# Delta rule on Trainium2: first convolution taps on ScalarE, query products on GpSimd, another order of late SiLUs

## The chip, the cores and the metric

The kernel runs on one core of a Trainium2 chip. The core has five engines that work side by side, each with its own instruction stream: TensorE (PE, matrix products into PSUM), VectorE (DVE), ScalarE (ACT, activation functions), GpSimd (POOL) and SyncE (SP, which here issues the transfers). They meet only at semaphores. The metric is the device time of one launch in microseconds (us), as the median over runs.

## What is computed

Two transformer-like blocks over 512 tokens of width 1024. The change sits in the first one, in front of its gated delta rule. There a projection gives queries, keys and values for eight heads of 128; each goes through a causal convolution of four taps over time and a SiLU; queries and keys are then brought to unit length.

```python
qkv = jax.nn.silu(causal_dwconv(jnp.concatenate([dn_q, dn_k, dn_v], axis=-1), dn_conv_w[l]))
q_a = l2_norm(qkv[..., :DN_QK].reshape(B, S, DN_HEADS, DN_DK))
k_a = l2_norm(qkv[..., DN_QK:2 * DN_QK].reshape(B, S, DN_HEADS, DN_DK))
v_a = qkv[..., 2 * DN_QK:].reshape(B, S, DN_HEADS, DN_DV)
...
o_a = gated_delta_rule(q_a, k_a, v_a, g_a, beta_a)
```

The delta rule works in chunks of 64 tokens. For each chunk and head a matrix `eye + a_mat` (unit lower triangular, made of the keys' products, their decay and beta) is inverted, then a state of 128x128 is carried from chunk to chunk, and the queries read it. Everything behind it (latent attention, the feed-forward part, the whole second block) needs its output.

## The kernel before, in words

Data stand transposed: channels on the 128 partitions, the 512 tokens along the free axis, so one head is one tile of 128x512. `ar` is an array of 50 such tiles; heads of Q are tiles 0 to 7, of K 8 to 15, of V 16 to 23. PSUM has eight banks of 128x512.

Projections. Weights come in panels of 128x2048, each of which serves two projections. SyncE loads a panel into `raw`, ScalarE makes its high part (`L1271`, "cast"), GpSimd the low part, the difference (`L2449`, four pieces, "split"), and each projection is 24 matmuls of 128x512, three for each of eight parts (`L398` to `L400`). There is room for two split panels; a panel's cast may start when TensorE has finished the panel two before. The functions `ahead` and `split` put these casts and splits into the streams of ScalarE and GpSimd in front of the first instruction that waits for a later step of TensorE: so where in a stream a wait on TensorE stands decides where a cast stands.

Convolutions. "Conv n" is the n-th in the order `QKV_ORDER`: n = 0 to 7 are keys, 8 to 15 queries, 16 to 23 values. VectorE computes it out of the bank of projection n: first tap `L1814` (a multiply by a column), three further taps `L1816`; the last one frees the bank. ScalarE then applies the SiLU in place (`conv_silu`, `L1402`), GpSimd squares the tile if n < 16 (`L2491`), TensorE sums the squares over the partitions (`L466`, the l2 sums), ScalarE takes logarithm and exponential of the sum (`rstds`, `L1335` and `L1338`), and VectorE multiplies (`unit_heads`, `L1943`), four heads a group: groups 0 and 1 are keys, 2 and 3 queries ("query products").

Beside this run the other parts of the delta rule. For t = 0 to 3 (pairs of chunks, "turns"), TensorE makes the running decays and the keys' products (`gb`, `kk`), VectorE masks them (`L1975`), ScalarE takes exponentials (`L1431`, `L1432`), VectorE multiplies (`L1983`), and conv 11 + t closes the turn. `unit_inverses` on VectorE inverts all 32x32 diagonal blocks at once: transposes in (`L1827`), 30 steps of two instructions (`L1836`, `L1837`) with other work woven in at every sixth step, copies, transposes back (`L1842`). Two masked products (`L2005`) hand the result to TensorE as XTR. `inverse_steps` then join 32x32 blocks to 64 and 128: x0 (transpose, TensorE `L656`, copied by ScalarE `L1448`), p5 (`L664`, copied `L1452`), x5 and xt5 (`L671`, `L675`, subtracted by VectorE), p6 and xt6, with GpSimd's masks (`L2505`, `L2506`, `L2509`) as further operands. Between two of these groups TensorE weaves three parts (nine matmuls) of projection 21 and later ones, and behind them the query-key products `kq`, which need all query products.

Banks. TensorE takes banks in turn out of a set: all eight first, only 0 to 5 while the inverses use 6 and 7. It may write a bank only when its last reader is done. By this turn the l2 sum of conv 10 falls on the bank of projection 15 (read by conv 15), that of conv 12 on the bank of projection 16, and projection 19 on the bank of projection 18.

The order of each stream is the order in which the code is written; nothing is reordered when it runs.

## Time and profile before

| | |
|---|---|
| median of 3 runs | 2207.74 us (2206.78 to 2209.82) |
| profiled execution | 2212.4 us, its span 2210.6 us |
| TensorE busy | 2060.6 us (93%) |
| VectorE busy | 935.7 us (42%) |
| GpSimd busy | 974.8 us (44%) |
| ScalarE busy | 798.7 us (36%) |
| mean granted clock of TensorE | 0.968 of full speed |

The page of the profile gives these for one execution, on the time axis of its span. Busy times overlap. Of the chain of work that ended last, TensorE has 83%, VectorE 9%, ScalarE 3% and GpSimd 2%. In the page's 40 slices of 55 us TensorE is busy for 9 tenths or more in most; the fourth and fifth slice (166 to 276 us), where the inverses and joining steps run, show 6 and 8 tenths, with a granted clock of 8 tenths in both. A wait is put down to the line that released it; the stretch of the change lies between 110 and 262 us.

### The profile page before, as it was taken

The numbers are of one execution on the slowest core, as the hardware profiler recorded it, in microseconds if no ns is written. First come the engines' busy times: TensorE is split into PE (matmuls) and PEld (weight loads), VectorE is DVE, ScalarE is ACT, GpSimd is POOL, SyncE is SP. The second block draws the span as 40 slices with busy tenths as digits, with TensorE's granted clock in tenths as the row PEclk, the third lists the DMA queues.
The fourth block names the chain that finished last, engine by engine and source line by source line (L and its number), as shares of the span: only waits on it lengthen the run. The fifth ranks groups of instructions, "written<-read, shape, count | busy, mean of one in ns | idle before, by whom it ended". The sixth has DMA issues, their size and how long they took to land.

```text
span 2210.6 us, 26367 instructions
## 1 busy us (share of the span) xinstructions
PE 2060.6 (93%) x10214; PEld 1652.1 (75%) x10214; DVE 935.7 (42%) x1531; ACT 798.7 (36%) x1049; POOL 974.8 (44%) x758
## 2 busy tenths in 40 slices
PE   6996899998999998999999798998999899999998
PEld 3684787785677886888888576875877687888886
DVE  2579545774543134222200577445943452111101
ACT  3454224236555234222222453333224643222221
POOL 3532442554312454655466364002442255555663
PEclk9998899999999999999999799998999999999999
DMA  6211104631101232222222311001222222222231
GB/s 286 77 51 45 39 20 163 231 125 57 53 32 50 96 134 76 97 98 102 103 98 101 119 58 58 2 30 58 96 76 77 76 93 80 97 101 103 84 113 76
DMA packets 25898, 194.96 MB, mean 88 GB/s; under 512 B 3120, under 2 KB 3376, under 8 KB 4912
## 3 DMA queue, kind: packets, MB, share of 16 engines
q1 hardware_dynamic: 25776, 193.29, 23.8%
q8 instruction: 82, 1.34, 0.2%
q14 instruction: 40, 0.33, 0.0%
HBM read 189.09 MB, written 4.19 MB: 87 GB/s over the span
## 4 chain that ended last, share of the span: by engine, by line
PE 83%; DVE 9%; ACT 3%; POOL 2%; issue 2%; DMA 1%; SPq 0%; ACTq 0%; DVEq 0%; POOLq 0%
PE ps L398 22%; PE ps L399 22%; PE ps L400 22%; PE ps L466 2%; POOL W L2449 2%; ACT W L1271 1%; PE ps L496 1%; DVE ar L1816 1%; PE ps L836 1%; PE ps L891 1%; DVE ar L1842 1%; PE ps L600 1%; PE ps L823 1%; DVE ar L1916 1%; DVE ar L1797 1%
## 5 line engine op out<-in xcount | busy, mean ns | idle before, releaser
L2449 POOL TENSOR_TENSOR W<-raw,W 128x512 fp32r<-128x512 f32 x588 | 775.4, 1319 | 1027.2 <-ACT W L1271 990.9
L398 PE MATMUL ps<-hH,W 128*128 128x512 f32 x1648 | 662.8, 402 | 48.7 <-DVE ar L1816 9.8
L400 PE MATMUL ps<-hH,W 128*128 128x512 f32 x1648 | 648.8, 394 | 0.0
L399 PE MATMUL ps<-arR,W 128*128 128x512 f32 x1392 | 543.5, 390 | 0.0
L1271 ACT CAST W<-raw 128x2048 fp32r<-128x2048 f32 x147 | 280.9, 1911 | 582.3 <-PE ps L400 554.9
L398 PEld LDWEIGHTS ps<-hH,W 128*128 128x128 f32 x1648 | 314.2, 191 | 134.0 <-issue 58.2
L400 PEld LDWEIGHTS ps<-hH,W 128*128 128x128 f32 x1648 | 314.1, 191 | 67.3
L399 PE MATMUL ps<-xL,W 128*128 128x512 f32 x848 | 337.0, 397 | 0.0
L399 PEld LDWEIGHTS ps<-arR,W 128*128 128x128 f32 x1392 | 262.4, 189 | 54.4 <-issue 0.2
L398 PE MATMUL ps<-arR,W 128*128 128x512 f32 x592 | 231.3, 391 | 3.3 <-DVE ar L1899 3.3
L400 PE MATMUL ps<-arR,W 128*128 128x512 f32 x592 | 230.9, 390 | 0.0
L399 PEld LDWEIGHTS ps<-xL,W 128*128 128x128 f32 x848 | 163.5, 193 | 33.8 <-issue 2.2
L398 PEld LDWEIGHTS ps<-arR,W 128*128 128x128 f32 x592 | 111.5, 188 | 27.3 <-DVE ar L1899 3.8
L400 PEld LDWEIGHTS ps<-arR,W 128*128 128x128 f32 x592 | 111.6, 188 | 23.3
L1816 DVE SCALAR_TENSOR_TENSOR ar<-ps,cols,ar 128x511 f32<-128x511 f32 (+1 forms) x130 | 97.4, 749 | 4.6
L466 PE MATMUL ps<-ar,cm 128*128 128x512 f32 x172 | 81.2, 618 | 13.8 <-DVE ar L1816 6.7
L1814 DVE TENSOR_SCALAR ar<-ps,cols 128x512 f32<-128x512 f32 x46 | 35.9, 779 | 105.7 <-PE ps L400 105.2
L1275 ACT CAST arR<-ar 128x512 fp32r<-128x512 f32 x74 | 45.9, 621 | 81.1 <-DVE ar L2420 31.3
L466 PEld LDWEIGHTS ps<-ar,cm 128*128 128x128 f32 x172 | 32.6, 196 | 53.8 <-issue 33.4
L1916 DVE SCALAR_TENSOR_TENSOR ar<-ar,st 128x512 f32<-128x512 f32 x56 | 59.3, 1058 | 2.0
L2414 DVE TENSOR_TENSOR ps<-ps,wide 128x512 f32<-128x512 f32 x22 | 15.4, 700 | 101.0 <-PE ps L400 88.4
L2418 DVE TENSOR_TENSOR ps<-ps,wide 128x512 f32<-128x512 f32 x22 | 15.4, 700 | 94.6 <-PE ps L400 94.6
(380 smaller groups left out, 2275.9 us busy)
## 6 DMA issues: line engine op xcount, KB each, us to landing
raw<-panels_dram SPq DMA_DIRECT2D x147, 1024.0 KB, 4.8
ar<-ada_dram SPq DMA_DIRECT2D x12, 2048.0 KB, 11.1
xT<-xT_dram SPq DMA_DIRECT2D x2, 2048.0 KB, 8.1
out_dram<-xT SPq DMA_DIRECT2D x8, 512.0 KB, 2.6
xT<-out_dram SPq DMA_DIRECT2D x1, 2048.0 KB, 7.7
wide<-wide_dram SPq DMA_DIRECT2D x1, 1024.0 KB, 4.8
cm<-cm_dram SPq DMA_DIRECT2D x1, 832.0 KB, 30.5
ar<-lora_dram SPq DMA_DIRECT2D x1, 512.0 KB, 3.2
```

The source lines that it names most:

```text
L398: mm(out, lhs[0], rhs[0], start=first, stop=False)
L399: mm(out, lhs[0], rhs[1], start=False, stop=False)
L400: return mm(out, lhs[1], rhs[0], start=False, stop=final)
L466: ins = mm(pst(name, i), sel[k] if isinstance(sel, list) else const(sel), sq, start=(k == 0), stop=(k == len(squares) - 1))
L496: ins = turn(pst((name, "turn", i))[:, c], tile(smt[i % 4])[:, c], const("ident"))
L600: ins = mm(heads4((what, t, hf))[:, h % HALF, :], tile(K0 + h)[:, c], tile((K0 if what == "kk" else Q0) + h)[:, c], start=True, stop=True)
L1271: link(nc.scalar.copy(W[:, n % SPLIT, 0, :], raw[:, n % RAW, :]), panel_high, n + 1)
L1275: link(nc.scalar.copy(dst, src), done, value)
L1814: link(ts(out, src, taps[-1], bias, ALU.mult, ALU.add if bias is not None else ALU.bypass))
L1816: ins = stt(out[:, j:S], src[:, 0:S - j], taps[n - 1 - j], out[:, j:S], ALU.mult, ALU.add)
L1916: ins = stt(acc, tile(ADA_BASE[i] + k), st[:, k:k + 1], acc, ALU.mult, ALU.add)
L2449: ins = tt(W[:, n % SPLIT, 1, c], raw[:, n % RAW, c], W[:, n % SPLIT, 0, c].bitcast(F32), ALU.subtract)
```

## The change

It does four things.

1. The first tap of conv 11 to 18 moves from VectorE to ScalarE (`conv_tap`, a multiply by a column, out of PSUM). VectorE's three further taps wait for it. Taps 11 to 14 stand at the end of the four turns; taps 15 and 16 behind SiLU 14; taps 17 and 18 one ahead of SiLU 17, one behind it.
2. The eight query products move from VectorE to GpSimd, behind its squares; between the fourth and fifth stands the split of a panel, and the split of the panel after that now comes behind the eighth, ahead of the masks, whose wait for the query products is gone.
3. On ScalarE the first query rates (logarithms and exponentials of group 2) now stand ahead of SiLU 16.
4. On ScalarE SiLU 19 and 20 now stand behind the joining steps' copies of x0 and p5, not ahead of them.

```diff
@@ -1403,6 +1403,11 @@
                     if n in SPLIT_AFTER:
                         ahead(act, "qkv", QKV_ORDER[n + 1])
 
+                def conv_tap(n):
+                    i = QKV_ORDER[n]
+                    filled(act, "qkv", i)
+                    link(nc.scalar.mul(tile(Q0 + i), pst("qkv", i), col("conv", 4 * i + 3)), sem("conv_tap"), n - 10)
+
                 def unit_rstds(g):
                     logarithm_next()
                     rstds("l2", range(4 * g, 4 * g + 4), (28, 29, 30, 31), 1.0, sem("l2_rstd"), sem("qk_normed"),
@@ -1430,16 +1435,22 @@
                         act.wait_ge(sem("gb_masked"), n)
                         link(af(pair(ATT + 2 * t, hf), pair(ATT + 2 * t, hf), ACT.Exp), sem("gdn_decay"), n)
                         link(af(spare(2 * t + hf), heads4(("gb", t, hf)), ACT.Exp), *read(("gb", t, hf)))
+                    conv_tap(11 + t)
                 act.wait_ge(sem("gc_dve"), 1)
                 link(af(sm4[:, EGC, :, :], sm4[:, GC, :, :], ACT.Exp))
                 link(af(sm4[:, KDEC, :, 0:8], sm4[:, KDEC, :, 0:8], ACT.Exp), sem("gc_act"), 1)
-                for n in range(11, 17):
+                for n in range(11, 15):
                     conv_silu(n)
+                conv_tap(15)
+                conv_tap(16)
+                conv_silu(15)
                 unit_rstds(2)
+                conv_silu(16)
+                conv_tap(17)
                 conv_silu(17)
+                conv_tap(18)
                 unit_rstds(3)
-                for n in range(18, 21):
-                    conv_silu(n)
+                conv_silu(18)
 
                 def inverse_steps(t):
 
@@ -1459,8 +1470,8 @@
                     yield
 
                 for n, _ in enumerate(inverse_steps(0)):
-                    if n == 3:
-                        conv_silu(21)
+                    if n in (0, 1, 3):
+                        conv_silu(19 + (n + 1) // 2)
                 for n, _ in enumerate(inverse_steps(1)):
                     if n == 1:
                         conv_silu(22)
@@ -1807,11 +1818,14 @@
                         else:
                             link(stt(dst(j), t, shift(j), h.bitcast(F32), ALU.add, ALU.subtract), *norm_step("low", name, j))
 
-            def causal_conv(job, i, out, taps, done, value, bias=None):
+            def causal_conv(job, i, out, taps, done, value, bias=None, tapped=None):
 
                 src = pst(job, i)
                 n = len(taps)
-                link(ts(out, src, taps[-1], bias, ALU.mult, ALU.add if bias is not None else ALU.bypass))
+                if tapped:
+                    dve.wait_ge(*tapped)
+                else:
+                    link(ts(out, src, taps[-1], bias, ALU.mult, ALU.add if bias is not None else ALU.bypass))
                 for j in range(1, n):
                     ins = stt(out[:, j:S], src[:, 0:S - j], taps[n - 1 - j], out[:, j:S], ALU.mult, ALU.add)
                     if j < n - 1:
@@ -1945,7 +1959,8 @@
                 def conv(n):
                     i = QKV_ORDER[n]
                     filled(dve, "qkv", i)
-                    causal_conv("qkv", i, tile(Q0 + i), [col("conv", 4 * i + j) for j in range(4)], None, None)
+                    causal_conv("qkv", i, tile(Q0 + i), [col("conv", 4 * i + j) for j in range(4)], None, None,
+                                tapped=(sem("conv_tap"), n - 10) if 11 <= n <= 18 else None)
 
                 for n in range(8):
                     conv(n)
@@ -1995,11 +2010,9 @@
                 conv(17)
                 for _ in range(6):
                     next(units)
-                unit_heads(2)
                 conv(18)
                 for _ in range(6):
                     next(units)
-                unit_heads(3)
                 next(units)
                 for hf in range(2):
                     link(tt(pair(XTR, hf), pair(AX, hf), bm(const("same32")), ALU.mult), sem("gdn_xtr"), 1 + hf)
@@ -2491,9 +2504,14 @@
                     link(tt(tile(24 + n % 4), x, x, ALU.mult), sem("l2_sq"), n + 1)
                     if n in SPLIT_AFTER:
                         ahead(pool, "qkv", QKV_ORDER[n + 1])
+                for n in range(8, 16):
+                    if n == 12:
+                        ahead(pool, "qkv", QKV_ORDER[18])
+                    pool.wait_ge(sem("l2_rstd"), n + 1)
+                    x = tile(Q0 + QKV_ORDER[n])
+                    link(tt(x, x, tile(28 + n % 4), ALU.mult), sem("qk_normed"), n + 1)
                 ahead(pool, "qkv", QKV_ORDER[19])
                 pool.wait_ge(consts_in, 16)
-                pool.wait_ge(sem("qk_normed"), 16)
                 pool.wait_ge(sem("ax_ready"), 1)
 
                 def masks(t):
```

GpSimd, from its last squares of the heads to its first masks (L2491 and L2504 squares, L2449 and L2462 splits, L2506 and L2524 masks), before:

```order
L2491 TENSOR_TENSOR ar<-ar 128x512 x4
L2449 TENSOR_TENSOR W<-raw,W 128x512 x8
L2506 TENSOR_TENSOR ar<-ar,cm 128x512 x2
L2509 TENSOR_TENSOR ar<-ar,cm 128x512 x2
L2449 TENSOR_TENSOR W<-raw,W 128x512 x4
L2505 TENSOR_TENSOR ar<-ar,cm 128x512
```

and now:

```order
L2504 TENSOR_TENSOR ar<-ar 128x512 x4
L2512 TENSOR_TENSOR ar<-ar 128x512 x4
L2462 TENSOR_TENSOR W<-raw,W 128x512 x4
L2512 TENSOR_TENSOR ar<-ar 128x512 x4
L2462 TENSOR_TENSOR W<-raw,W 128x512 x4
L2524 TENSOR_TENSOR ar<-ar,cm 128x512 x2
L2527 TENSOR_TENSOR ar<-ar,cm 128x512 x2
L2462 TENSOR_TENSOR W<-raw,W 128x512 x4
```

L2512 are the query products, four and four, with one panel's split between them and one behind them; before, both splits stood together.

ScalarE, from SiLU 13 and 14 on to the second group of query rates (L1402 SiLU, L1325 table for logarithms, L1335 and L1338 rates, L1271 cast), before:

```order
L1271 CAST W<-raw 128x2048
L1402 ACTIVATE ar<-ar 128x512 x2
L1325 ACT_TABLE_LOAD
L1335 ACTIVATE ar<-ps,cols 128x512 x4
L1338 ACTIVATE ar<-ar,cols 128x512 x4
L1271 CAST W<-raw 128x2048
L1402 ACT_TABLE_LOAD
L1402 ACTIVATE ar<-ar 128x512
L1325 ACT_TABLE_LOAD
L1335 ACTIVATE ar<-ps,cols 128x512 x4
L1338 ACTIVATE ar<-ar,cols 128x512 x4
```

and now (L1409 is the tap):

```order
L1402 ACTIVATE ar<-ar 128x512 x4
L1271 CAST W<-raw 128x2048
L1409 ACTIVATE ar<-ps,cols 128x512 x2
L1402 ACTIVATE ar<-ar 128x512
L1325 ACT_TABLE_LOAD
L1335 ACTIVATE ar<-ps,cols 128x512 x4
L1338 ACTIVATE ar<-ar,cols 128x512 x4
L1402 ACT_TABLE_LOAD
L1402 ACTIVATE ar<-ar 128x512
L1271 CAST W<-raw 128x2048
L1409 ACTIVATE ar<-ps,cols 128x512
L1402 ACTIVATE ar<-ar 128x512
```

Two taps follow the cast, the rates of group 2 come behind one SiLU instead of two, and the next cast stands in front of tap 17.

ScalarE, from the SiLU of conv 18 to the first joining steps (L1448 and L1459 copies of x0, L1452 and L1463 of p5, L1457 and L1468 of p6), before:

```order
L1402 ACT_TABLE_LOAD
L1402 ACTIVATE ar<-ar 128x512
L1271 CAST W<-raw 128x2048
L1402 ACTIVATE ar<-ar 128x512 x2
L1448 COPY ar<-ps 128x512 x2
L1452 COPY ar<-ps 128x512 x2
L1271 CAST W<-raw 128x2048
L1457 COPY ar<-ps 128x512 x2
```

and now:

```order
L1325 ACT_TABLE_LOAD
L1335 ACTIVATE ar<-ps,cols 128x512 x4
L1338 ACTIVATE ar<-ar,cols 128x512 x4
L1402 ACT_TABLE_LOAD
L1402 ACTIVATE ar<-ar 128x512
L1271 CAST W<-raw 128x2048
L1459 COPY ar<-ps 128x512 x2
L1402 ACTIVATE ar<-ar 128x512
L1463 COPY ar<-ps 128x512 x2
```

The SiLUs of conv 19 and 20 stood both ahead of the copies of x0; now one stands behind these and one behind those of p5.

## Rows read from the trace of the kernel before

**Rows 1.** Waits of TensorE, 165 to 262 us: total us, times, longest us

```profile
PE ps L398 <- DVE ar L1816: 9.8, 1, 9.8
PE ps L466 <- DVE ar L1816: 6.7, 1, 6.7
PE ps L656 <- DVE ar L2005: 4.3, 2, 3.3
PE ps L664 <- ACT ar L1448: 3.3, 1, 3.3
```

**Rows 2.** Timeline of VectorE, 165 to 219 us: start, us, line, operation

```profile
165.05 2.32 DVE L1816 SCALAR_TENSOR_TENSOR ar<-ps,cols,ar 128x511 f32<-128x511 f32 x3
...
180.81 0.75 DVE L1814 TENSOR_SCALAR ar<-ps,cols 128x512 f32<-128x512 f32 x1
...
186.67 0.38 DVE L1837 TENSOR_TENSOR ps<-ps,ar 128x210 f32<-128x210 f32 x1
...
197.24 0.75 DVE L1814 TENSOR_SCALAR ar<-ps,cols 128x512 f32<-128x512 f32 x1
...
202.49 0.38 DVE L1837 TENSOR_TENSOR ps<-ps,ar 128x210 f32<-128x210 f32 x1
...
205.22 4.33 DVE L1943 TENSOR_TENSOR ar<-ar 128x512 f32<-128x512 f32 x4
...
210.38 2.32 DVE L1816 SCALAR_TENSOR_TENSOR ar<-ps,cols,ar 128x511 f32<-128x511 f32 x3
...
216.24 2.87 DVE L1943 TENSOR_TENSOR ar<-ar 128x512 f32<-128x512 f32 x4
```

**Rows 3.** Chain that ended last, the masked products: start, us, what

```profile
228.75 0.70 DVE ar L2005
229.48 1.65 DVE ar L2005
```

**Rows 4.** Timeline of TensorE, 194 to 247 us

```profile
194.68 2.84 PE L466 MATMUL ps<-ar,cm 128*128 128x512 f32 x6 [1.01 <-ACT ar L1335]
...
212.84 0.77 PE L398 MATMUL ps<-hH,W 128*128 128x512 f32 x1 [9.84 <-DVE ar L1816]
...
225.82 0.39 PE L400 MATMUL ps<-hH,W 128*128 128x512 f32 x1
...
231.94 0.78 PE L398 MATMUL ps<-hH,W 128*128 128x512 f32 x1
...
238.79 3.78 PE L664 MATMUL ps<-ar 128*128 128x128 f32 x16 [3.31 <-ACT ar L1448]
...
245.59 1.06 PE L671 MATMUL ps<-ar 128*128 128x128 f32 x8
```

**Rows 5.** Timeline of ScalarE, 162 to 238 us

```profile
162.17 0.60 ACT L1432 ACTIVATE trig<-ps 128x512 f32<-128x512 f32 x1
...
192.65 1.28 ACT L1325 ACT_TABLE_LOAD   x1
193.94 2.85 ACT L1335 ACTIVATE ar<-ps,cols 128x512 f32<-128x512 f32 x4
...
199.85 1.92 ACT L1271 CAST W<-raw 128x2048 fp32r<-128x2048 f32 x1
...
237.49 0.63 ACT L1402 ACTIVATE ar<-ar 128x512 f32<-128x512 f32 x1 [2.50 <-DVE ar L1816]
```

**Rows 6.** Timeline of GpSimd, 222 to 272 us

```profile
222.90 5.37 POOL L2449 TENSOR_TENSOR W<-raw,W 128x512 fp32r<-128x512 f32 x4 [15.35 <-ACT W L1271]
228.89 3.36 POOL L2506 TENSOR_TENSOR ar<-ar,cm 128x512 f32<-128x512 f32 x2 [0.61 <-DVE ar L1842]
...
271.30 2.65 POOL L2518 TENSOR_TENSOR ar<-ar,wide 128x512 f32<-128x512 f32 x2
```

**Rows 7.** Stretches: busy us of PE, PEld, DVE, ACT, POOL, then granted clock

```profile
242.00:246.00 4.00, 4.00 (x16) 3.33 (x16) 0.00 (x0) 0.59 (x1) 1.56 (x2) 0.65 0.00 0
```

**Rows 8.** Chain that ended last, a panel load

```profile
420.85 10.44 DMA raw<-panels_dram
```

## The prediction

> **What bounds the kernel now.** I read the page first: TensorE is busy nearly throughout, so time is to be had only where it waits. The view of waits, cut to the stretch of the change, gives those: between 165 and 262 us TensorE stands 9.8 and 6.7 us for the convolution line of VectorE, 4.3 us for the masked products behind VectorE's inverse, and 3.3 us for a ScalarE copy [rows 1]. The timelines say what stands behind each. VectorE works from 165 to 231 without a pause: conv 14, the transposes, the 30 steps of the 32x32 inverses with conv 15 to 18 and eight query products between them, the transposes back, two masked products [rows 2, 3]. Conv 15 frees the bank of the third l2 sum (the 6.7 us), conv 18 that of projection 19 (the 9.8 us, which end at 212.84), and the masked products release x0 [rows 2, 4]. Then ScalarE: its copy of x0, for which TensorE waits until 238.79, stands behind the SiLU of conv 19 and 20, the second of which begins at 237.49, after VectorE's conv 20 [rows 4, 5]. So the chain is VectorE's until 231, then passes between VectorE, ScalarE and TensorE.
>
> **The change on VectorE.** Its chain behind conv 14 loses four first taps (conv 15 to 18) at 0.75 us and 0.04 to the next instruction, 3.15 us, and the query products of group 2, 4.33 us, and of group 3, 2.87 us, with 0.07 for the gaps [rows 2]. Together 10.4 us.
>
> What it pays: conv 11 to 14 now wait for a tap on ScalarE. No row shows such a tap; the nearest are an exponential from PSUM without a column (0.60) and logarithms from PSUM with one (2.85 for four, 0.71) [rows 5]. I take 0.70, as the tap has a column; the bounds differ by 0.1 us a tap. The order puts a panel cast of 1.92 us [rows 5] ahead of the taps of conv 11 and 13, and both cast and tap can start only when TensorE has done that projection. These two convs end 1.9 us later. That heals in the turn behind each, since VectorE waited some 1.3 us for the next projection and there is no cast ahead of taps 12 and 14. Tap 14 starts when ScalarE's last copy of the turn (162.17 + 0.60, now 1.9 us later) is done, at 164.65, and ends at 165.35; the other three taps of conv 14 start at 165.4 against 165.05 [rows 2, 5]. Late by 0.4 us. TensorE takes up no bank in between that these convs still hold. VectorE's chain is shorter by 10.4 - 0.4 = 10.0 us.
>
> Do the later taps come in time? Behind tap 14 ScalarE has two small exponentials (0.5), a table load (1.28) and four SiLUs (0.65 with the gap) [rows 5], 169.8 us, then a cast: taps 15 and 16 are done by 172.5 and 176.3, and VectorE wants them at 181.2 and 188.4. Tap 17 is the tight one. ScalarE has SiLU 15 (conv 15 now ends at 183.5), a table, four logarithms and four exponentials (193.94 to 199.85 before, 5.9), a table and SiLU 16, until 193.4; then the cast that the tap pulls ahead of itself (1.92), and the tap: 196.0. VectorE wants it at 197.24 - 1.2 = 196.0 [rows 2, 5]. I take 0.1 us; each us that ScalarE is later is a us on the chain. Tap 18 needs projection 18, which ends at 201.4 (now without the wait of 1.0 us in the sums before it [rows 4], as the logarithms stand ahead of SiLU 16); it is done at 202.2 and wanted at 203.3. So conv 18 ends at 205.6 instead of 212.7 [rows 2], and TensorE's 9.8 us become 4.3. The inverse is back at 218.7 instead of 228.75 [rows 3].
>
> **The change on GpSimd.** It gets eight products. The nearest product of two tiles in place takes 1.33 us (2.65 for two); beside VectorE two mask products took 1.68 each (3.36) [rows 6]. I take 1.33; 1.68 moves nothing: the first four run from 189.2 to 194.5 and then wait for the panel cast anyway, and the last four, behind the exponentials at 207, end at 212.3 (213.7 at 1.68), while their reader (kq) stands behind projection 21. But the order puts the split of the next panel (5.37 us [rows 6]) ahead of the masks, and its cast waits for projection 19. Projections 19 and 20 ran from 212.84 to 226.2, the second at full clock, 24 matmuls at 0.23, so the first took 7.8 us [rows 4]: now until 213.4. Cast until 215.5, split until 221.0, GpSimd's masks at 222.8 and 224.1. Before, they began beside the end of the inverse, at 228.89 [rows 6].
>
> This split now runs beside VectorE's two masked products. Before, the first took 0.70 alone and the second 1.65 beside GpSimd [rows 3]; four query products beside GpSimd took 4.33 against 2.87 without [rows 2]. So 1.3 and 1.65: they end at 220.0 and 221.6, 9.5 us earlier than before, not 10.0. The steps of the inverse do not suffer: one of 210 columns took 0.38 us at 202.49, beside a split, and at 186.67 [rows 2].
>
> The Trainium skill has one rule for both (SBUF — State Buffer, "Who interferes with whom"): a VectorE instruction with two SBUF inputs and a GpSimd instruction that reads SBUF lock each other out, one with a single SBUF input does not. By that rule, with each masked product locked out for a whole GpSimd product of 1.3 us, the pair would take 4 us, and a further us of the gain would go; the trace agrees on which instructions suffer, and on the size I go by its row of four.
>
> **The change on ScalarE behind the inverse.** SiLU 19 and 20 now follow the copies of x0 and p5, and the 3.3 us go [rows 1]. What is late next: x0's second half starts at 221.7 and takes 0.6, the nine woven matmuls of projection 21 take 2.1 at 0.23 [rows 4]; TensorE is at p5 at 224.4, GpSimd's second mask is ready at 224.1. No new wait, by a hair.
>
> **The clock.** Behind its waits TensorE runs slower: the granted clock of 242 to 246 is 0.65 [rows 7]. From 231.94 to 245.59 it took 13.65 us, 3.3 of them waiting; eighteen woven matmuls at 0.23 (4.1) and p5's sixteen at 2.0 (two of the groups of eight that start at 245.59, 1.06 each, less their overlap) would be 6.1: 4.3 us lost to the clock [rows 4]. Instead of waits of 4.3 and 3.3 us there are now two of 1 us. Behind one of 1.01 us six matmuls took 2.84, which is full speed [rows 4]. None or all of the 4.3 come back; I take 3.5, near the row of 1.01.
>
> **The sum.** Masked products 9.5, ScalarE's wait 3.3, clock 3.5: 16.3 us by the group at 245.59. Bounds: with none of the clock 12.8, with all of it 17.1; with tap 17 a us late and GpSimd's mask a us late besides 10.8; with the masked products unhindered and a shorter ramp behind the shorter wait before projection 19, 19. Behind this everything hangs on the same chain: casts follow projections, masks follow casts. ScalarE's 10.4 us for a panel at 420.85 [rows 8] too: that panel is queued behind large loads that SyncE issues when the last outputs of the delta rule are done. So the gain stays. The profiled execution took 2212.4 us (span 2210.6 and 1.8 around it), so 2196.1; the median of the runs, 2207.7, lies 4.7 lower, so 2191.4.
>
> **Rivals.** (1) GpSimd takes the place of the wait removed: its masks come 3 to 5 us behind the inverse, TensorE waits 2 us for them before p5 and falls back to the low clock: 9.5 + 3.3 - 2, about 11 us, 2197. For it speaks the margin of 0.3 us; against it that every term ahead of the masks is a row. (2) ScalarE becomes the bound: taps 17 and 18 come some 4 us late behind the cast and the table, conv 18 and all behind it as well, and with the ramp about 8 us remain without most of the clock: 2200. For it: tap 17 has no margin. (3) The change does not do what it says, because the gain is given back: if the load queue set the wait at 420.85, up to 10.4 us go, and with rival 1 nothing measurable is left: 2207. Against it: the order of the queue ties the load to the delta rule. (4) Slower: GpSimd's serial chain of eight products, two splits and masks sets the end. It costs a us for each us by which the second mask is later than 224.4, and decides from 16.3 us on; then the last four products would take over 5 us each, and for 2212, slower by 0.2%, 6.3 each. Rows give 1.33 to 1.68.
>
> **How the numbers follow.** Forecast 0.73, with a range of its own of 2188 to 2195; rival 1 0.13, rival 2 0.08, rival 3 0.03, rival 4 0.03. The range, 2187 to 2199, leaves out rivals 3 and 4, half of rival 2 and a few in a hundred below. 0.2% (4.4 us) is about what can be told from no change: faster by more 0.94, within it 0.03, slower 0.03.
>
> **What would show it.** TensorE's wait for conv 18 is 4 to 5 us instead of 9.8, that for conv 15 stays at 6 to 7, that for the copy of x0 is gone, the transposes back end near 218.7, and VectorE waits for no tap from conv 15 on by more than 0.5 us. Wrong would be: a wait of TensorE for GpSimd's masks before p5 (rival 1), pauses of VectorE before conv 17 or 18 (rival 2), a longer wait for the panel near 405 (rival 3).

## The result, and the profile after

The changed kernel takes 2193.7 us in the median of six runs (2186.4 to 2197.3), the kernel before beside it 2208.9 us (2206.8 to 2212.9): a ratio of 0.992, with a 95% interval of 0.9904 to 0.9935. The forecast was 2191.4 us, and the gain of the medians is 15.2 us where 16.3 were forecast. In a later set of runs (c_after, below) the same kernel was 23.3 us faster than the kernel before beside it, so one set gives the gain only to within some us. The profiled execution took 2191.7 us against 2212.4, its mean granted clock 0.973 against 0.968. The page's first rows of after:

```profile
span 2189.8 us, 26374 instructions
...
PE 2052.5 (94%) x10214; PEld 1646.1 (75%) x10214; DVE 924.2 (42%) x1515; ACT 804.3 (37%) x1057; POOL 982.8 (45%) x766
```

TensorE's busy time fell by 8 us although its work is the same; the rest of the gain is waits. Waits of TensorE in the kernel after, 165 to 250 us (total us, times, longest us; L1830 is the convolution line that was L1816, L2018 the masked products that were L2005):

```profile
PE ps L466 <- DVE ar L1830: 6.4, 1, 6.4
PE ps L398 <- DVE ar L1830: 4.4, 1, 4.4
...
PE ps L656 <- DVE ar L2018: 2.3, 2, 1.3
```

Of the four waits of [rows 1], 9.8 became 4.4, 6.7 is 6.4, the 4.3 of the masked products are 2.3, and the 3.3 for ScalarE's copy are gone. The timeline of VectorE after (start, us, line, operation, in brackets the idle time before and its releaser; "..." marks rows left out), beside [rows 2, 3]:

```profile
139.61 2.32 DVE L1830 SCALAR_TENSOR_TENSOR ar<-ps,cols,ar 128x511 f32<-128x511 f32 x3 [3.46 <-ACT ar L1409]
...
147.22 2.31 DVE L1830 SCALAR_TENSOR_TENSOR ar<-ps,cols,ar 128x511 f32<-128x511 f32 x3 [0.70 <-ACT ar L1409]
...
157.71 2.32 DVE L1830 SCALAR_TENSOR_TENSOR ar<-ps,cols,ar 128x511 f32<-128x511 f32 x3 [3.57 <-ACT ar L1409]
...
165.32 2.31 DVE L1830 SCALAR_TENSOR_TENSOR ar<-ps,cols,ar 128x511 f32<-128x511 f32 x3 [0.70 <-ACT ar L1409]
...
181.10 2.32 DVE L1830 SCALAR_TENSOR_TENSOR ar<-ps,cols,ar 128x511 f32<-128x511 f32 x3
...
196.07 2.32 DVE L1830 SCALAR_TENSOR_TENSOR ar<-ps,cols,ar 128x511 f32<-128x511 f32 x3 [0.16 <-ACT ar L1409]
...
203.27 2.31 DVE L1830 SCALAR_TENSOR_TENSOR ar<-ps,cols,ar 128x511 f32<-128x511 f32 x3
...
210.57 8.29 DVE L1856 STREAM_TRANSPOSE ar<-ar 32x1024 f32<-32x1024 f32 x4
218.89 3.18 DVE L2018 TENSOR_TENSOR ar<-ar,cm 128x512 f32<-128x512 f32 x2
```

The first four rows are conv 11 to 14: behind a panel cast they wait 3.5 us for their tap, without one 0.7, and conv 14 starts 0.3 us later than in [rows 2] (0.5 later by the mark used below). Conv 15 waits for nothing, conv 17 for 0.16 us, conv 18 for nothing. The transposes back start at 210.57, and the two masked products take 3.18 us. ScalarE after, with tap 14, the first query rates, the cast and tap 17, the cast of the panel behind projection 19, and the first copy of x0:

```profile
164.50 0.69 ACT L1409 ACTIVATE ar<-ps,cols 128x512 f32<-128x512 f32 x1
...
185.45 2.85 ACT L1335 ACTIVATE ar<-ps,cols 128x512 f32<-128x512 f32 x4
...
193.31 1.91 ACT L1271 CAST W<-raw 128x2048 fp32r<-128x2048 f32 x1
195.25 0.69 ACT L1409 ACTIVATE ar<-ps,cols 128x512 f32<-128x512 f32 x1
...
213.78 1.91 ACT L1271 CAST W<-raw 128x2048 fp32r<-128x2048 f32 x1 [2.50 <-issue]
...
222.87 0.59 ACT L1459 COPY ar<-ps 128x512 f32<-128x512 f32 x1 [1.09 <-PE ps L656]
```

A tap takes 0.69 us. The copy of x0 at 222.87 waits for TensorE alone; in [rows 5] a SiLU of conv 20 still began at 237.49. GpSimd after, with the two groups of query products, the split and the masks, beside [rows 6]:

```profile
189.20 5.40 POOL L2512 TENSOR_TENSOR ar<-ar 128x512 f32<-128x512 f32 x4 [0.99 <-ACT ar L1338]
...
207.22 5.38 POOL L2512 TENSOR_TENSOR ar<-ar 128x512 f32<-128x512 f32 x4 [6.46 <-ACT ar L1338]
215.83 5.69 POOL L2462 TENSOR_TENSOR W<-raw,W 128x512 fp32r<-128x512 f32 x4 [3.24 <-ACT W L1271]
221.60 2.98 POOL L2524 TENSOR_TENSOR ar<-ar,cm 128x512 f32<-128x512 f32 x2
```

A product takes 1.35 us, and the masks end at 224.58. TensorE after, the second half of x0, p5 and x5, beside [rows 4]:

```profile
222.12 0.66 PE L656 MATMUL ps<-cm,ar 128*128 128x128 f32 x4 [1.02 <-DVE ar L2018]
...
224.69 1.95 PE L664 MATMUL ps<-ar 128*128 128x128 f32 x16
...
228.53 1.05 PE L671 MATMUL ps<-ar 128*128 128x128 f32 x8
```

p5 starts at once and takes 1.95 us (3.78 before), x5 starts at 228.53 instead of 245.59.

To compare runs I put time zero at TensorE's products ahead of the transposes in (169.4 us in the trace before, 169.2 after). The last column is one TensorE instruction far on, in block 2 at about 1235 us.

| kernel | transposes back start | masked products: start, us | x5 starts | block 2 |
|---|---|---|---|---|
| before | 51.16 | 59.32, 2.37 | 76.16 | 1066.13 |
| after | 41.37 | 49.69, 3.18 | 59.33 | 1049.12 |
| difference | 9.79 | 9.63 | 16.83 | 17.01 |

So the whole gain is made by x5 and none is given back behind it: behind 262 us every wait of TensorE has its old length within 0.3 us, the load of the panel of [rows 8] took 10.53 us, and the lead stays at 17 to 17.5 us until 1684 us. The two profiled executions differ by 20.8 us because of two steps more, of 1.6 us each, in the attention of block 2. There the trace before has two stretches at a low clock (busy us of PE, PEld, DVE, ACT, POOL, then granted clock, DMA share, GB/s):

```profile
1701.00:1709.00 8.00, 6.87 (x38) 5.03 (x38) 2.64 (x12) 3.60 (x11) 0.00 (x0) 0.79 0.16 68
1726.00:1734.00 8.00, 7.01 (x40) 5.05 (x41) 2.51 (x10) 3.62 (x11) 0.00 (x0) 0.79 0.08 35
```

and the trace after, in the same work 17.6 us earlier, none:

```profile
1683.40:1691.40 8.00, 6.44 (x48) 4.67 (x50) 3.01 (x12) 4.51 (x13) 0.00 (x0) 1.00 0.15 63
1708.40:1716.40 8.00, 7.07 (x54) 4.97 (x53) 3.19 (x11) 4.43 (x12) 0.00 (x0) 1.00 0.01 2
```

A second profiled execution of the kernel after, unchanged (label c_after), has them again, with a span of 2193.2 us against 2189.8:

```profile
1680.00:1700.00 20.00, 17.31 (x118) 12.67 (x117) 8.12 (x31) 11.35 (x26) 0.76 (x2) 0.91 0.14 54
1700.00:1720.00 20.00, 17.32 (x109) 13.03 (x109) 8.16 (x23) 9.71 (x27) 5.21 (x4) 0.91 0.15 54
```

One kernel has them in one execution and not in another, so they are not part of the change. I take them for a part of the spread between runs (2186 to 2197 us); what sets them off stays open.

A third such place lies close behind x5, at the second of x0's two groups of the second turn, where TensorE waits 2.0 us for GpSimd in most of the traces. In the trace after, the matmuls behind that wait run at the low clock, in the trace of e7 (below) behind the same wait they do not:

```profile
245.25 1.11 PE L656 MATMUL ps<-cm,ar 128*128 128x128 f32 x4 [2.03 <-POOL ar L2523]
246.42 0.66 PE L656 MATMUL ps<-cm,ar 128*128 128x128 f32 x4 [2.02 <-POOL ar L2523]
```

The granted clock over the 4 us from 245 was 0.62 in after, and 1.00 over the 4 us from 246 in e7. From x5 of the first turn to p5 of the second it took 21.7 to 22.0 us in seven traces (before, after, c_after, e2, e3, e4, e8) and 20.4 us in six (e1, e5, e6, e7, e9, e11). So a trace can gain or lose 1.5 us there that its edit has not made. Behind the instruction in block 2 the fourteen traces take from 967.6 us (e9) to 976.2 us (e7) to their end, with the same instructions. That is why the experiments are read at x5 first and by their times second.

### The profile page after: what moved, and what is told of

Same layout as the page of the kernel before. It is cut to its first block, busy times and chain, and to the rows that moved or that the text cites. A ratio compares the mean times of both kernels' runs of the same rounds, so it can differ in the third digit from the quotient of the medians.

```text
span 2189.8 us, 26374 instructions
## 1 busy us (share of the span) xinstructions
PE 2052.5 (94%) x10214; PEld 1646.1 (75%) x10214; DVE 924.2 (42%) x1515; ACT 804.3 (37%) x1057; POOL 982.8 (45%) x766
## 4 chain that ended last, share of the span: by engine, by line
PE 82%; DVE 9%; ACT 4%; POOL 2%; issue 2%; DMA 1%; SPq 0%; ACTq 0%; DVEq 0%; POOLq 0%
PE ps L398 22%; PE ps L399 21%; PE ps L400 21%; PE ps L466 2%; POOL W L2462 1%; ACT W L1271 1%; PE ps L496 1%; PE ps L836 1%; DVE ar L1830 1%; PE ps L891 1%; DVE ar L1856 1%; PE ps L823 1%; DVE ar L1930 1%; PE ps L600 1%; DVE ar L1808 1%
## 5 line engine op out<-in xcount | busy, mean ns | idle before, releaser
L2462 POOL TENSOR_TENSOR W<-raw,W 128x512 fp32r<-128x512 f32 x588 | 773.6, 1316 | 996.8 <-ACT W L1271 960.5
L1271 ACT CAST W<-raw 128x2048 fp32r<-128x2048 f32 x147 | 280.9, 1911 | 575.2 <-PE ps L400 550.8
L1830 DVE SCALAR_TENSOR_TENSOR ar<-ps,cols,ar 128x511 f32<-128x511 f32 (+1 forms) x130 | 97.3, 749 | 13.0 <-ACT ar L1409 8.6
L1828 DVE TENSOR_SCALAR ar<-ps,cols 128x512 f32<-128x512 f32 x38 | 29.8, 785 | 100.8 <-PE ps L400 100.5
```

The costliest lines, as they stand in the source:

```text
L1271: link(nc.scalar.copy(W[:, n % SPLIT, 0, :], raw[:, n % RAW, :]), panel_high, n + 1)
L1828: link(ts(out, src, taps[-1], bias, ALU.mult, ALU.add if bias is not None else ALU.bypass))
L1830: ins = stt(out[:, j:S], src[:, 0:S - j], taps[n - 1 - j], out[:, j:S], ALU.mult, ALU.add)
L2462: ins = tt(W[:, n % SPLIT, 1, c], raw[:, n % RAW, c], W[:, n % SPLIT, 0, c].bitcast(F32), ALU.subtract)
```

## The experiments

Twelve runs, in three sets of four, each timed beside the kernel before on the same chip (2210.8, 2211.8 and 2211.4 us). "Ratio" is to before, with its 95% interval. The last two columns are differences to after, + where the run comes later; for e5 they are to before.

| label | median us | ratio | x5 starts | x5, difference | block 2, difference |
|---|---|---|---|---|---|
| e1_late_ahead | 2201.1 | 0.9949 (0.9934 to 0.9964) | 66.59 | +7.26 | +6.74 |
| e2_products_dve | 2200.4 | 0.9945 (0.9929 to 0.9962) | 65.78 | +6.45 | +7.16 |
| e3_taps_dve | 2194.7 | 0.9925 (0.9908 to 0.9942) | 61.54 | +2.21 | +3.11 |
| e6_rates_behind | 2198.8 | 0.9951 (0.9931 to 0.9970) | 63.81 | +4.48 | +3.72 |
| e4_taps_15_18 | 2190.4 | 0.9905 (0.9890 to 0.9920) | 58.99 | -0.34 | +0.54 |
| e5_late_only | 2198.1 | 0.9946 (0.9927 to 0.9965) | 69.69 | -6.47 | -7.63 |
| e7_mask_twice | 2193.8 | 0.9924 (0.9902 to 0.9947) | 59.94 | +0.61 | +0.13 |
| e11_mask_late | 2197.9 | 0.9939 (0.9926 to 0.9953) | 63.71 | +4.38 | +3.45 |
| e8_masks_first | 2188.0 | 0.9905 (0.9881 to 0.9929) | 57.55 | -1.78 | -0.73 |
| e9_both | 2185.6 | 0.9890 (0.9875 to 0.9905) | 57.00 | -2.33 | -2.70 |
| e10_xtr_first | 2186.4 | 0.9890 (0.9876 to 0.9903) | 57.02 | -2.31 | -6.64 |
| c_after | 2188.0 | 0.9902 (0.9887 to 0.9917) | 59.35 | +0.02 | +0.24 |

Between x5 and block 2 all differences but that of e10 change by 0.2 to 1.2 us, which is no more than the place with two outcomes above can do.

**Each part undone.** e1_late_ahead puts SiLU 19 and 20 back ahead of the copies.

```diff
...
+                conv_silu(19)
+                conv_silu(20)
...
-                    if n in (0, 1, 3):
-                        conv_silu(19 + (n + 1) // 2)
+                    if n == 3:
+                        conv_silu(21)
```

> The changed kernel with part 4 undone: SiLU 19 and 20 stand ahead of the copies of x0 again. My account: SiLU 20 waits for conv 20, which now ends at 228.4, so the copies of x0 end at 229.7, TensorE waits some 5 us before p5 (224.7 now) and falls back to the low clock for p5 and the woven matmuls (3 us more): the group x5 starts at 236.6 instead of 228.5, 8 us later, and the whole is 2201 to 2202. Rival (GpSimd's masks hold p5 anyway): at most 1 us. Rival (the wait goes but the clock is none of its business): 5 us.

Measured: 7.26 us later, where 8 were expected. Waits of TensorE in e1:

```profile
PE ps L664 <- ACT ar L1461: 4.9, 1, 4.9
PE ps L398 <- DVE ar L1832: 3.6, 1, 3.6
```

The wait for ScalarE's copy is back, now 4.9 us, and p5 took 3.78 us again, as at the low clock before [rows 4]. The granted clock was 0.50 over the 4 us from p5 on. The masked products ended within 0.1 us of after's, so beyond the wait itself 2.3 us are clock. They ended there although VectorE's transposes back started 0.7 us later than in after (42.09 against 41.37); the run of e11 below has the same, and shows why.

e2_products_dve gives VectorE its eight products again.

```diff
...
+                unit_heads(2)
...
+                unit_heads(3)
...
-                for n in range(8, 16):
-                    if n == 12:
-                        ahead(pool, "qkv", QKV_ORDER[18])
-                    pool.wait_ge(sem("l2_rstd"), n + 1)
-                    x = tile(Q0 + QKV_ORDER[n])
-                    link(tt(x, x, tile(28 + n % 4), ALU.mult), sem("qk_normed"), n + 1)
...
+                pool.wait_ge(sem("qk_normed"), 16)
```

> The changed kernel with part 2 undone: the eight query products are back on VectorE, the taps stay on ScalarE. My account: each group costs VectorE 2.9 us when no split runs beside it, so conv 18 ends 2.9 us later, the inverse 5.8 us, and x5 starts at 234 to 235 (228.5 now), plus up to 1 us of clock: 2199 to 2201. Rival (ScalarE's taps bound VectorE, so products in between are free): 0 to 1 us. Rival (products beside a split as before, 4.3 and 2.9): 7.2 us.

Measured: 6.45 us later. VectorE in e2, the two groups of products and the masked products:

```profile
203.58 2.87 DVE L1957 TENSOR_TENSOR ar<-ar 128x512 f32<-128x512 f32 x4
...
212.33 2.87 DVE L1957 TENSOR_TENSOR ar<-ar 128x512 f32<-128x512 f32 x4
...
224.86 2.36 DVE L2020 TENSOR_TENSOR ar<-ar,cm 128x512 f32<-128x512 f32 x2
```

2.87 us for each group, 5.7 together; the transposes back start 5.83 us later. The masked products took 2.36 us, which gives 0.8 back, and behind them 1.6 us are lost. TensorE in e2 shows where:

```profile
225.60 0.66 PE L656 MATMUL ps<-cm,ar 128*128 128x128 f32 x4 [3.04 <-DVE ar L2020]
...
228.07 0.63 PE L399 MATMUL ps<-xL,W 128*128 128x512 f32 x1
...
231.42 1.95 PE L664 MATMUL ps<-ar 128*128 128x128 f32 x16
```

It waited 3.04 us for the first masked product (1.31 in after), and the second of the nine matmuls woven in behind x0 took 0.63 us, as did most of the others; in after they take 0.39. That is the clock: 0.73 over 227 to 229 us, and 1.00 over 222 to 228 us in after.

e3_taps_dve gives the eight first taps back to VectorE.

```diff
...
-                    conv_tap(11 + t)
...
-                conv_tap(15)
-                conv_tap(16)
...
-                conv_tap(17)
...
-                conv_tap(18)
...
-                                tapped=(sem("conv_tap"), n - 10) if 11 <= n <= 18 else None)
+                                tapped=(sem("conv_tap"), n - 10) if False else None)
```

> The changed kernel with part 1 undone: all first taps on VectorE. My account: the four taps of conv 15 to 18 come back into the chain, 3.15 us, less the 0.3 us by which conv 14 is late now and 0.1 of waiting for tap 17: the masked products and x5 come 2.8 us later, 2196 to 2197. Rival (ScalarE's taps and casts cost what they give): 0.

Measured: 2.21 us later, where 2.8 were expected. The transposes back start 2.53 us later, and the masked products take 2.37 us instead of 3.18, which gives 0.8 back. VectorE's masked products and GpSimd's split in e3:

```profile
221.54 2.37 DVE L2013 TENSOR_TENSOR ar<-ar,cm 128x512 f32<-128x512 f32 x2
218.97 6.07 POOL L2457 TENSOR_TENSOR W<-raw,W 128x512 fp32r<-128x512 f32 x4 [7.57 <-ACT W L1271]
```

They lie inside the split, as in after, and yet take 0.8 us less: it matters where in the split they begin. The split takes 6.07 us for 5.69, the second mask is ready at 227.77, and p5's second half waits 0.22 us for it; between p5's start and x5 0.5 us is lost.

e6_rates_behind puts the first query rates back behind SiLU 16.

```diff
...
+                conv_silu(16)
...
-                conv_silu(16)
```

> The changed kernel with part 3 undone: SiLU 16 ahead of the query rates of group 2. My account: the rates then wait for conv 16 (190.6 us) and a SiLU, are done at 198.4, the cast and tap 17 come behind them at 201.0 instead of 195.9; conv 17, conv 18 and the inverse are 5 us later, x5 at 233.5: 2198 to 2199. Rival (tap 17 has slack that I did not see): 0 to 1 us.

Measured: 4.48 us later. VectorE in e6, conv 17:

```profile
202.09 2.32 DVE L1830 SCALAR_TENSOR_TENSOR ar<-ps,cols,ar 128x511 f32<-128x511 f32 x3 [5.41 <-ACT ar L1409]
```

It waits 5.41 us for its tap. So tap 17 had no margin, as the forecast said, and part 3 is worth something only because of it: 5.3 us at the transposes back, of which 0.8 come back in the masked products, which again meet the split at another point (2.37 us, from 224.89, beside a split from 221.03 to 226.70). The four losses of e1, e2, e3 and e6 add up to 20.4 us, the change to 16.8: its parts overlap.

**One part alone.** e5_late_only is the kernel before with the two SiLUs moved and nothing else.

```diff
...
-                for n in range(18, 21):
-                    conv_silu(n)
+                conv_silu(18)
...
-                    if n == 3:
-                        conv_silu(21)
+                    if n in (0, 1, 3):
+                        conv_silu(19 + (n + 1) // 2)
```

> The kernel before with part 4 alone: SiLU 19 and 20 behind the copies of x0 and p5. My account: the wait of 3.3 us before p5 goes (x0 and its copy are done by 233, the woven matmuls end at 235.5, GpSimd's masks at 232), and with it most of the low clock behind it, 3 us: x5 starts at 239 to 240 instead of 245.6, 6.3 us. Rival (only the wait, the clock stays low from the wait for the masked products): 3.3 us, x5 at 242.3. Rival (another wait takes its place): 0 to 1.

Measured: x5 6.47 us earlier than before, with VectorE's chain exactly where it was. TensorE in e5:

```profile
228.70 0.66 PE L656 MATMUL ps<-cm,ar 128*128 128x128 f32 x4 [3.38 <-DVE ar L2004]
230.37 1.12 PE L656 MATMUL ps<-cm,ar 128*128 128x128 f32 x4 [1.02 <-DVE ar L2004]
...
234.48 1.95 PE L664 MATMUL ps<-ar 128*128 128x128 f32 x16
...
238.32 1.05 PE L671 MATMUL ps<-ar 128*128 128x128 f32 x8
```

No wait ahead of p5, and p5 at 1.95 us instead of 3.78 [rows 4]. The wait itself was 3.3 us [rows 1]; the other 3.2 are clock. A wait of 3.38 us for the masked products still stands in front of x0, and from their end to x5 e5 takes 8.00 us, after 6.46: 1.5 us, as in e2, belong to that wait. So moving two SiLUs brings twice what the view of waits shows for it. The medians of e5 say more, 13.7 us, nearly as much as the whole change in its first set: in its trace the same work behind block 2 takes 969.1 us against 975.0 before, with a granted clock of 0.92 against 0.86 over the first 160 us of it. No run shows that the edit does this, so I do not count it for the SiLUs.

**Fewer taps moved.** e4_taps_15_18 leaves the first taps of conv 11 to 14 on VectorE, where each was hidden before the change.

```diff
...
-                    link(nc.scalar.mul(tile(Q0 + i), pst("qkv", i), col("conv", 4 * i + 3)), sem("conv_tap"), n - 10)
+                    link(nc.scalar.mul(tile(Q0 + i), pst("qkv", i), col("conv", 4 * i + 3)), sem("conv_tap"), n - 14)
...
-                    conv_tap(11 + t)
...
-                                tapped=(sem("conv_tap"), n - 10) if 11 <= n <= 18 else None)
+                                tapped=(sem("conv_tap"), n - 14) if 15 <= n <= 18 else None)
```

> The changed kernel with taps 11 to 14 back on VectorE, taps 15 to 18 on ScalarE. My account: conv 14 ends 0.3 us earlier and all of the chain with it: x5 at 228.2 instead of 228.5, in the runs no difference. Rival (the waits of 3.5 us for taps 11 and 13 cost more than that later on): 1 us or more faster. Rival (tap 17 is held by the cast, not by conv 15): 0.

Measured: x5 0.34 us earlier. The transposes in start at -2.03 as before, not -1.54: the late conv 14 cost 0.5 us. In block 2 nothing is left of it (0.54 us later than after), and the median, 2190.4 us, does not decide it.

**The margin of GpSimd's masks.** e7_mask_twice makes the first of them one product longer.

```diff
...
+                        if t == 0 and hf == 0:
+                            link(tt(pair(MK, hf), pair(AX + 2 * t, hf), bm(const("lvl5")), ALU.mult))
```

> The changed kernel in which GpSimd makes its first mask product of the first turn twice, to delay its masks by 1.3 to 1.7 us. My account (the masks are ready just as TensorE comes to p5, no slack): p5 and x5 start 1.3 to 1.6 us later, the clock stays up: x5 at 230.0. Rival (the masks have slack): 0. Rival (a longer wait also drops the clock): 3 us or more.

Measured: 0.61 us later, where 1.3 to 1.6 were expected: a miss. TensorE in e7, the halves of p5:

```profile
225.34 1.12 PE L664 MATMUL ps<-ar 128*128 128x128 f32 x8
226.68 1.13 PE L664 MATMUL ps<-ar 128*128 128x128 f32 x8 [0.23 <-issue]
```

The second mask came at 226.59, after p5's start at 225.34, and held up only p5's second half, by 0.23 us: that half alone reads it. The margin was about a microsecond, not "a hair".

e11_mask_late repeats that product three times, to make the wait certain.

```diff
...
-                        if t == 0 and hf == 0:
+                        for _ in range(3 if t == 0 and hf == 0 else 0):
```

> The changed kernel in which GpSimd makes its first mask product of the first turn four times, to delay its masks by some 3.9 us (one product more moved x5 by only 0.6 us, so the slack is 0.7). My account: TensorE waits 3.2 us before p5, as it did for ScalarE in the kernel before, and loses another 2.5 to 3 us to the low clock of p5 and the woven matmuls: x5 5.5 to 6 us later than in the changed kernel. Rival (the low clock there came from the earlier waits, not from this one): 3.2 us.

Measured: 4.38 us later, where 5.5 to 6 were expected; the first mask was ready at 226.56 us, the second at 227.91. TensorE in e11, p5:

```profile
226.67 3.58 PE L664 MATMUL ps<-ar 128*128 128x128 f32 x16 [2.51 <-issue]
```

The wait is 2.51 us (3.2 expected), and p5 takes 3.58 instead of 1.95; the granted clock over 226 to 230 us was 0.57. The masked products ended when after's did, so the loss is 2.5 us of wait and 1.9 of clock. That is rival 1 made true.

This trace also differs from after where its edit does nothing, ahead of the masks. Conv 17, the masked products and GpSimd's split in e11:

```profile
196.02 2.32 DVE L1830 SCALAR_TENSOR_TENSOR ar<-ps,cols,ar 128x511 f32<-128x511 f32 x3 [0.81 <-ACT ar L1409]
218.83 2.53 DVE L2018 TENSOR_TENSOR ar<-ar,cm 128x512 f32<-128x512 f32 x2
215.14 5.67 POOL L2462 TENSOR_TENSOR W<-raw,W 128x512 fp32r<-128x512 f32 x4 [1.83 <-ACT W L1271]
```

Conv 17 waits 0.81 us for tap 17, not 0.16: behind the wait for conv 15 TensorE stayed at the low clock for longer (0.50 over the 3 us from 17 us behind time zero, 0.93 in after), and the panel cast ahead of the tap came 0.7 us later. VectorE's chain comes 0.7 us later by it, here and in e1. The masked products end no later, because they take 2.53 us instead of 3.18. In both kernels they end 0.55 us behind the split: 221.36 behind 220.81 here, 222.07 behind 221.52 in after.

**Masks and masked products ahead of the split.** In e8_masks_first the split of the panel behind projection 19 follows GpSimd's first masks, and these wait for VectorE's masked products.

```diff
...
-                ahead(pool, "qkv", QKV_ORDER[19])
...
+                pool.wait_ge(sem("gdn_xtr"), 2)
...
+                    if t == 0:
+                        ahead(pool, "qkv", QKV_ORDER[19])
```

> The changed kernel with the split of the last value panel behind GpSimd's first two masks, which wait for VectorE's masked products. My account: the masked products take 1.4 us without company instead of 3.2, the transposes back 7.7 instead of 8.3: x0 and x5 start 2.0 to 2.3 us earlier, x5 at 226.3. Rival (the split is then late for projection 22 or for the later masks): TensorE waits as much elsewhere, 0 or slower. Rival (only the order of casts matters): 0.

Measured: 1.78 us earlier. VectorE in e8, the transposes back and the masked products:

```profile
210.10 8.23 DVE L1856 STREAM_TRANSPOSE ar<-ar 32x1024 f32<-32x1024 f32 x4
218.37 1.42 DVE L2018 TENSOR_TENSOR ar<-ar,cm 128x512 f32<-128x512 f32 x2
```

The pair takes 1.42 us without a neighbour; the transposes take 8.23 us, no less than beside the split, where 7.7 were expected. In block 2 only 0.73 us of the gain is left. At x5 of the fourth turn it is still 2.4 us, so the rest goes behind the inverses, and where was not settled.

e9_both takes e8 and e4 together.

> The changed kernel with taps 11 to 14 back on VectorE, and the last value panel's split behind GpSimd's first two masks, which wait for the masked products. My account: the two gains add up, x5 2.1 us earlier than in the changed kernel. Rival (part is lost again in the joining steps behind, as 1 us was when only the masks were moved): 1 us at block 2.

Measured: -2.33 us at x5, where e8 and e4 give -2.12 together: there the gains add. In block 2 it is -2.70, where those of e8 and e4 give -0.19; the trace of e9 is one of those that keep the full clock behind the wait of 2.0 us in the second turn, which is 1.5 us of it, and the rest is open. Its median, 2185.6 us (2184.3 to 2188.6), is the lowest of all, 2.4 below c_after beside it (2186.9 to 2195.0); the runs of the two overlap.

e10_xtr_first is e9 with one line more: in the later turns both of GpSimd's XTR products come ahead of its masks, not in turn with them.

```diff
...
+                    for hf in range(2):
```

> As the one before, and on GpSimd both masked copies for x0 (XTR) of a turn ahead of both masks for p5. My account: the second x0 of turns 1 and 3 waits for the second copy, which comes 1.3 us earlier; 2.6 us less of waiting, and up to 1 us of clock in the kq products behind: 3 us faster than the one before. Rival (p5 then waits for its masks): 0.

TensorE in e10, the second turn's x0:

```profile
239.25 0.66 PE L656 MATMUL ps<-cm,ar 128*128 128x128 f32 x4 [0.57 <-POOL ar L2522]
240.59 0.65 PE L656 MATMUL ps<-cm,ar 128*128 128x128 f32 x4 [0.69 <-POOL ar L2522]
```

x0's second half waits 0.69 us instead of 2.0, and block 2 is 3.9 us earlier than in e9. The runs don't show it (2186.4 against 2185.6 us, where 3 us faster was expected: a miss). The two traces tell where it goes: behind block 2 e10 takes 975.8 us and e9 967.6 for the same work, with a granted clock of 0.87 against 0.92 over the first 160 us of it. Whether that follows from the edit is open.

c_after is the changed kernel again.

> The changed kernel itself, beside the next three and the kernel before. My account: x5 starts 59.3 us behind the unit-block products as in its first trace, within 0.1; the time is 16 to 20 us under the kernel before, and its runs spread by some us with stretches of low clock that fall at other places in every kernel. Rival (the extra 3.5 us of the first trace over the 17.3 are part of the change): the late stretch of block 2 is again 3.5 us shorter than before's.

Measured: x5 at 59.35 against 59.33. The column can't always be read as finely as that: e1 and e11 had VectorE's chain 0.7 us later for nothing in their edits. The median of its runs, 2188.0 us, lies 5.7 below that of the first six and 23.3 below the kernel before beside it, where 16 to 20 were expected: a miss. Its stretch behind block 2 takes 974.7 us, in the trace before 975.0, in the first trace after 971.5; so the extra 3.5 us of that trace are no part of the change.

## Why the prediction was right

**The sum.** 16.8 us were found by x5 and 16.3 forecast, but two terms were off and made up for each other:

| term | forecast | measured |
|---|---|---|
| masked products end earlier | 9.5 | 8.8 |
| ScalarE's wait | 3.3 | 3.3 |
| clock | 3.5 | 4.7 |
| given back behind x5 | 0 | 0 |

**VectorE's chain.** Its steps held: a tap of 0.70 (0.69), conv 14 late by 0.4 (0.5 from the mark), tap 17 done at 196.0 (195.94) with 0.1 us of waiting (0.16), TensorE's wait for conv 18 at 4.3 (4.4), the transposes back done at 218.7 (218.86). So the transposes back came 9.79 us earlier where the forecast had 10.0. e2 shows 5.8 of it as the products' 2.87 twice. The forecast had booked 4.33 for the first group, what it took beside GpSimd's split in the trace before; in e2 it did not meet that split, and e2 loses 1.4 us less than the change had removed.

**The masked products.** This is the term that was mis-sized: 9.5 forecast, 8.8 measured, with the pair at 2.95 us (1.3 and 1.65) where it took 3.18, and 3.34 in e4, against 2.37 before. The forecast gave each product a price for its company. The runs show that the company alone does not fix it: the pair takes 1.42 us without any (e8), and beside a split anything from 2.37 (e3, e6) over 2.53 and 2.58 (e11, e1) to 3.18 and 3.34 (after, e4). What holds in every trace is that a masked product begun while a GpSimd product runs ends 0.54 to 0.59 us after that one does; in after, e1, e4, e6 and e11 the second ends 0.55 us behind the split. So in the changed kernel GpSimd's split sets the end of the pair, and with it x0. It also means that the forecast's "each us that ScalarE is later is a us on the chain" is too strict: in e1 and e11 0.7 us of it cost 0.1 at most. The Trainium skill (SBUF — State Buffer, "Who interferes with whom") says that a VectorE instruction with two SBUF inputs and a GpSimd instruction that reads SBUF lock each other out for a whole instruction; the runs agree, but what a product loses is the rest of the GpSimd product that it meets, so the 4 us that a whole one for each would have given lie above all that was measured. They also agree that a transpose, with one input, doesn't suffer (8.23 and 8.29 us).

**ScalarE and the clock.** The wait of 3.3 us went entirely. From the end of the masked products to x5 it took 14.47 us before and 6.46 after: 8.0 less, 3.3 of it the wait and 4.7 clock. The forecast counted with 4.3 from x0 on and took 3.5 of it, not all; all of it came back, in p5 (3.78 to 1.95), the matmuls woven in, and the second half of x0 (1.12 to 0.66). The runs divide it: 3.2 hang on the wait ahead of p5 (e5 against before; e11 and e1 lose 1.9 and 2.3 with such a wait put back), and 1.5 on the wait of 3.0 to 3.4 us ahead of x0, which the shorter chain of VectorE cut to 1.31 (e5 and e2 against after). Each of these is one trace, and the two are not quite independent: a wait ahead of p5 costs 3.2 where one stands ahead of x0 too, and 1.9 to 2.3 where none does. The forecast had only one lump for both.

**GpSimd.** Its products and the split came as forecast (1.35 each, masks ready at 224.58 for 224.1), TensorE at p5 at 224.69 for 224.4, and there was no wait. The reasoning of the margin was wrong: the forecast compared the second mask with p5's start, where only p5's second half reads it (e7). That made rival 1 look nearer than it was. The split that stands ahead of the masks is also what the masked products meet, which the forecast had seen.

**The rivals.** Rival 1 (masks late) and rival 2 (tap 17 and 18 late) did not come to pass; e11 and e6 made each true, for 4.4 and 4.5 us, where the forecast put them 5.3 and 8.3 us behind itself. Rival 3 (the panel wait takes it) fell: that wait moved along whole, and the lead did not change across it. Rival 4 would have needed products of over 5 us; they take 1.35.

**The forecast time.** 2191.4 was 2207.7 less 16.3. The six runs put before at 2208.9 and after at 2193.7; of the 2.3 us between forecast and median, 1.2 is the base and 1.1 the gain, both less than the runs of either kernel spread. That 2191.4 came so near is in part luck: beside its own runs of before, c_after gained 23.3 us. The evidence for the account is x5 in the traces, 16.8 us for 16.3.

## What to carry to other kernels

A short wait in a stretch with few matmuls costs more than the view of waits shows: price it by comparing the matmuls behind it with the same ones at full speed, and look for the instruction that stands ahead of the awaited copy for no reason. Work moved to an idle engine is paid where the two engines then run side by side, so ask which instruction will be its neighbour and when each begins, and put the one on the chain first. Margins are to be counted to the instruction that reads the data, not to the start of its group.

## What the runs showed that I had not expected

The pair of masked products costs from 1.42 to 3.34 us, by whether GpSimd runs beside it and by where in a GpSimd product each begins; in the changed kernel its end follows GpSimd's split and not VectorE's own chain. A wait of 2.5 to 4.9 us ahead of x0 or p5 costs another 1.5 to 3.2 us in clock behind it, while those of 1.0 to 1.3 us that after has ahead of x0 are followed by matmuls at full speed (p5 1.95 us). One of 2.0 us in the second turn was followed by either, and where the clock fell it cost 1.5 us. And the same kernel, run twice, has low-clock stretches of about 1.6 us cost each in the attention of block 2 in one execution and none in the other.
